# Levels 8, 16 and 32 of a block inverse: full 128x128 products against two alternating products on the diagonal 64x64 blocks

## Chip, cores and metric

One core of one Trainium2 chip. The metric is device time in microseconds of one execution, the median over the runs. The kernel computes one block of a hybrid model (a gated delta rule mixer and a convolution mixer, an output projection, a hierarchical mixture of experts, a gated embedding) over 1024 tokens of 1024 channels, all in f32 outside of a few f32r and f16 products.

## The reference, cut to what matters

The part that the change touches is the gated delta rule. For each chunk of tokens and each of 4 heads (key and value width 128) it needs the inverse of a unit lower triangular matrix:

```python
L = jnp.where(strict, jnp.einsum('bhncd,bhnsd->bhncs', k_beta, k) * decay, 0.0)
Tm = lax.linalg.triangular_solve(L + eye, eye, left_side=True, lower=True, unit_diagonal=True)
u = jnp.einsum('bhncs,bhnse->bhnce', Tm, v_beta)
w = jnp.einsum('bhncs,bhnsd->bhncd', Tm, k_beta * jnp.exp(gc)[..., None])
...
def step(S, xs_n):
    u_n, w_n, qk_n, qd_n, kd_n, gt_n = xs_n
    v_new = u_n - jnp.einsum('bhcd,bhde->bhce', w_n, S)
    o_n = jnp.einsum('bhcd,bhde->bhce', qd_n, S) + jnp.einsum('bhcs,bhse->bhce', qk_n, v_new)
    S = S * gt_n[..., None, None] + jnp.einsum('bhcd,bhce->bhde', kd_n, v_new)
    return S, o_n
```

## The kernel before

The kernel is a row of blocks that follow each other: the norm and the input projection with the two convolutions (to about 350 us), preparations of the decays, the delta rule (the block of lines 712 to 1311), the output projection with the routers (from line 1357), the routing, the experts (line 1560 on), and the last gate and norm. All engines of a block have ended before the next block begins. Within a block each engine has its own list of instructions, written out in order by hand, and they wait for each other through semaphores whose steps have names (`Steps`, line 22).

The delta rule works on tiles of 128 tokens, in 4 pairs of two tiles (g = 0, 1); every step is done for g = 0 and then for g = 1, on 4 heads at a time: an operand is `[128, 4, 128]`, and a result fills one bank of PSUM, `A[g][0]` or `A[g][1]` for the inverse, `Bk[0]` to `Bk[3]` for the rest. The inverse X of (1 + L) and its transpose Y are built up. Blocks of 8x8 are inverted column by column on VectorE (`eliminate`, line 1021), then the size of the inverted diagonal blocks is doubled level by level. Level l (3, 4, 5 for blocks of 8, 16, 32) takes ml, the part of L under the diagonal blocks that the level joins (masked by GpSimd, line 878), and does:

- U: `A[g][1] = ml^T X` on TensorE (`level_u`, line 1165), copied to `U[g]` by ScalarE (`kept`, line 786);
- X: `A[g][0] = Y^T U` (`level_x`, line 1180), and on VectorE X = X - A (`level`, line 1030);
- Y: `A[g][1] = U^T Y` (`level_y`, line 1187), and Y = Y - A on VectorE (the same function).

All matrices of these three levels have nothing outside of the two diagonal 64x64 blocks. At level 5 X is already computed for the first 64x64 block alone, since only that block of X is read afterwards. Level 6 joins the two 64x64 blocks with products of one 64x64 corner (U6, Y6), which lie partly in rows or columns 64 to 127 of the array.

PE's order for a pair is in `levels` (line 1245): U3, the turn (transpose) of the next pair's keys for g = 0, X3, Y3, the turn of the keys for g = 1, U4, X4, Y4, the turns of the queries, U5, the turns of the values, X5, Y5, KK (keys by keys of the next pair), U6, QK, Y6. Then come the solve and the state: read_state (kS), solve (of R), change (of ve), read_out, for g = 0 and 1. Line 1131 is the helper in which all these matmuls are recorded, so in the trace they are told apart by their tiles (`ps_ga<-X,ml` is U, `ps_ga<-U,Y` is X, `ps_ga<-Y,U` is Y of a level). The last pair has no next one, and so neither turns nor KK nor QK.

ScalarE's order for a pair (`levels`, line 825): U3 copies, the next keys' copies and squares (16 instructions of squares and sums), U4 copies, SiLU of the next queries and values, U5 copies, squares of the queries, U6, Y6. VectorE's order (line 1080): the subtractions of level 3, small norms, level 4, the scaled values, level 5, then on the next pair corners (d from KK, reduce, E), products (QKT, LT), the start of X8, and norm_columns; then R of the solve (line 1044).

Of the kernel before, what the change touches and what calls it, by code (L numbers as in the profile page):

```python
# [5 lines left out]
P = 128  # L6
# [5 lines left out]
ALU = mybir.AluOpType  # L12
ACT = mybir.ActivationFunctionType
# [32 lines left out]
def hybrid_block_kernel(nc, x, p, g_mix, w_in, w_conv_qkv, a_log, dt_bias, g_gdn_out, b_glu,  # L46
# [4 lines left out]
    H, DK = a_log.shape[1], g_gdn_out.shape[1]  # L51
# [24 lines left out]
    def psum(name, shape, dt=F32, ctx=None):  # L76
        return (ctx or top).enter_context(nc.psum_tensor(name, shape, dt))

    def sem(name):
        return top.enter_context(nc.semaphore(name))  # L80
# [14 lines left out]
    with top:  # L95
# [597 lines left out]
        CK = [slice(0, P // 2), slice(P // 2, P)]  # L693
        LV = (3, 4, 5)

        def both(*names):
            return [f"{n}{g}" for n in names for g in G2]

        p_one = Steps(sem("pe_one"), both("tk", "tq", "tv", "KK", "QK") + ["LR"] + both("Y8"))
        p_two = Steps(sem("pe_two"), both("U3", "X3", "Y3", "U4", "X4", "Y4", "U5", "X5", "Y5", "U6", "Y6")  # L700
                      + [f"{n}{g}" for g in G2 for n in ("kS", "AR", "dS", "o")] + both("ty"))
        a_one = Steps(sem("act_one"), both("silk", "kt", "sqk", "silq", "silv", "sqq", "y8"))
        a_two = Steps(sem("act_two"), both("U3", "U4", "U5", "U6", "Y6") + ["zs0", "zs1", "ln"]
                      + [f"va{g}" for g in G2] + both("sqo"))
        elim = [f"{n}{m}" for m in range(BS - 1, 0, -1) for n in ("et", "ex")]
        v_one = Steps(sem("dve_one"), ["ms", "rc", "bk"] + both("vb") + ["eq"] + both("c8", "cr") + ["ee"] + both("qk", "lt") + ["ec"] + elim)
        v_two = Steps(sem("dve_two"), both("X3", "Y3", "X4", "Y4", "X5", "Y5") + ["nrm"]
                      + [f"{n}{g}" for g in G2 for n in ("R", "ve", "S")] + both("on", "y"))
# [3 lines left out]
        with ExitStack() as c4:  # L712
            def two(name, shape=F4):
                return [sb(f"{name}_{g}", shape, ctx=c4) for g in G2]
# [5 lines left out]
            LT, d8, kg, X, Y, U = (two(n) for n in ("LT", "d8", "kg", "X", "Y", "U"))  # L720
            on = d8
            ml = [two(f"ml{s}") for s in G2]
# [6 lines left out]
            A = [[psum(f"ps_ga{g}{n}", F4, ctx=c4) for n in G2] for g in G2]  # L729
# [20 lines left out]
            def _(act):  # L750
# [35 lines left out]
                def kept(i, l):  # L786
                    for g in G2:
                        act.wait_ge(*p_two.sem_at(f"U{l}{g}", i))
                        if l == 3 and i:
                            act.wait_ge(*a_two.sem_at(f"sqo{g}", i - 1))  # L790
                        if l < 6:
                            nc.scalar.activation(U[g][:], A[g][1][:], ACT.Copy).then_inc(*a_two(f"U{l}{g}"))
                        else:
                            nc.scalar.activation(U[g][CK[1], :, CK[0]], A[g][0][CK[1], :, CK[1]], ACT.Copy).then_inc(*a_two(f"U{l}{g}"))

# [29 lines left out]
                def levels(i, ahead):  # L825
                    kept(i, 3)
                    if ahead:
                        keys(i + 1)
                        squares(i + 1, "k")
                    kept(i, 4)  # L830
                    if ahead:
                        turned(i + 1, "q")
                        turned(i + 1, "v")
                    kept(i, 5)
                    if ahead:
                        squares(i + 1, "q")
                    kept(i, 6)
                    corner(i)
                    gates_and_norm(i)
# [121 lines left out]
            def _(dve):  # L961
# [68 lines left out]
                def level(i, l):  # L1030
                    for g in G2:
                        dve.wait_ge(*p_two.sem_at(f"X{l}{g}", i))
                        r = (slice(0, P), slice(0, P)) if l < 5 else (CK[0], CK[0])
                        nc.vector.tensor_tensor(X[g][r[0], :, r[1]], X[g][r[0], :, r[1]], A[g][0][r[0], :, r[1]], ALU.subtract).then_inc(*v_two(f"X{l}{g}"))
                    for g in G2:
                        dve.wait_ge(*p_two.sem_at(f"Y{l}{g}", i))
                        nc.vector.tensor_tensor(Y[g][:], Y[g][:], A[g][1][:], ALU.subtract).then_inc(*v_two(f"Y{l}{g}"))

                def norm_columns(i):
                    cols = slice(2 * P * i, 2 * P * (i + 1))  # L1040
# [39 lines left out]
                def levels(i, ahead):  # L1080
                    level(i, 3)
                    if ahead:
                        norms(i + 1)
                    level(i, 4)
                    if ahead:
                        values(i + 1)
                    level(i, 5)
                    if ahead:
                        query_norms(i + 1)
                        corners(i + 1)  # L1090
                        products(i + 1)
                        start_blocks(i + 1)
                    norm_columns(i)
# [30 lines left out]
            def _(pe):  # L1124
                def heads(f):
                    for h in range(H):
                        last = f(h)
                    return last

                def mm(out, a, b, start=True, stop=True):  # L1130
                    return nc.tensor.matmul(out, a, b, start=start, stop=stop)

                def turn(i, c, g):
                    n = "qkv".index(c)
                    pe.wait_ge(*a_one.sem_at(f"sil{c}{g}", i))
                    if c == "v":
                        pe.wait_ge(*a_one.sem_at(f"kt{g}", i))
                        pe.wait_ge(*a_one.sem_at(f"sqk{g}", i))
                    elif i == 1:
                        pe.wait_ge(*v_one.sem_at(f"{'qk' if c == 'k' else 'lt'}{g}", 0))  # L1140
                    elif i:
                        pe.wait_ge(*v_two.sem_at(f"{'y' if c == 'k' else 'on'}{g}", i - 2))
                    bank = Bk[2 + g] if c == "q" else Bk[g]
                    heads(lambda h: nc.tensor.transpose(bank[:, h], qkvs[g][:, H * n + h], ident[:])).then_inc(*p_one(f"t{c}{g}"))
# [20 lines left out]
                def level_u(i, l, g):  # L1165
                    if l == 6:
                        pe.wait_ge(*v_two.sem_at(f"X5{g}", i))
                        heads(lambda h: mm(A[g][0][CK[1], h, CK[1]], LT[g][CK[0], h, CK[1]], X[g][CK[0], h, CK[0]])).then_inc(*p_two(f"U6{g}"))
                        return
                    if l == 3:  # L1170
                        pe.wait_ge(*g_one.sem_at(f"m3{g}", i))
                        if i:
                            pe.wait_ge(*a_two.sem_at(f"Y6{g}", i - 1))
                    else:
                        pe.wait_ge(*(g_one.sem_at(f"m4{g}", i) if l == 4 else g_two.sem_at(f"m5{g}", i)))
                        pe.wait_ge(*v_two.sem_at(f"X{l - 1}{g}", i))
                        pe.wait_ge(*v_two.sem_at(f"Y{l - 1}{g}", i))
                    heads(lambda h: mm(A[g][1][:, h], ml[1 if l == 4 else 0][g][:, h], X[g][:, h])).then_inc(*p_two(f"U{l}{g}"))

                def level_x(i, l, g):  # L1180
                    pe.wait_ge(*a_two.sem_at(f"U{l}{g}", i))
                    if l == 3:
                        pe.wait_ge(*a_one.sem_at(f"y8{g}", i))
                    r = (slice(0, P), slice(0, P)) if l < 5 else (CK[0], CK[0])
                    heads(lambda h: mm(A[g][0][r[0], h, r[1]], Y[g][r[0], h, r[1]], U[g][r[0], h, r[1]])).then_inc(*p_two(f"X{l}{g}"))

                def level_y(i, l, g):
                    if l == 6:
                        pe.wait_ge(*a_two.sem_at(f"U6{g}", i))
                        pe.wait_ge(*v_two.sem_at(f"Y5{g}", i))  # L1190
                        heads(lambda h: mm(A[g][1][CK[0], h, CK[0]], U[g][CK[1], h, CK[0]], Y[g][CK[1], h, CK[1]])).then_inc(*p_two(f"Y6{g}"))
                        return
                    heads(lambda h: mm(A[g][1][:, h], U[g][:, h], Y[g][:, h])).then_inc(*p_two(f"Y{l}{g}"))

                def read_state(i, g):
                    pe.wait_ge(*g_one.sem_at(f"kg{g}", i))
# [48 lines left out]
                def levels(i, ahead):  # L1245
                    n = i + 1
                    level_u(i, 3, 0)
                    level_u(i, 3, 1)
                    if ahead:
                        turn(n, "k", 0)  # L1250
                    level_x(i, 3, 0)
                    level_x(i, 3, 1)
                    level_y(i, 3, 0)
                    level_y(i, 3, 1)
                    if ahead:
                        turn(n, "k", 1)
                    level_u(i, 4, 0)
                    level_u(i, 4, 1)
                    level_x(i, 4, 0)
                    level_x(i, 4, 1)  # L1260
                    level_y(i, 4, 0)
                    level_y(i, 4, 1)
                    if ahead:
                        turn(n, "q", 0)
                        turn(n, "q", 1)
# [1114 lines left out]
```

## Time and profile before

| what | us |
|---|---|
| median of 3 runs | 1468.87 |
| runs | 1466.95 to 1472.25 |
| the profiled execution, its own time | 1466.72 |
| its span | 1465.0 |
| PE busy | 1191.1 |
| VectorE busy | 630.3 |
| ScalarE busy | 320.4 |
| GpSimd busy | 243.2 |

Times in the rows are us from the start of the span, durations of one instruction ns. PE is TensorE's matmul, PEld its weight load, which overlaps matmuls; DVE is VectorE, ACT ScalarE, POOL GpSimd. `out<-in` names the tiles, the shape behind it is rows*columns of the array in use and the size of the moving operand, xN the number of instructions. The busy time of a merged row reaches from the first start to the last end. PEclk is the granted share of the 2.4 GHz clock. A bracket at the end says how long the engine was idle before, and whom it waited for.

### The profile page before, as it was taken

What the parts mean: (1) busy time and instruction counts of PE and PEld (TensorE: products, weight loads), DVE (VectorE), ACT (ScalarE), POOL (GpSimd) and SP (SyncE); (2) the same over time, 40 slices, a digit from 0 to 9 for tenths busy, and PEclk for the clock granted to TensorE, in tenths of its full rate; (3) what the DMA queues carried; (4) which work ended last, traced back from release to release, by engine and by line L of the source; (5) the groups of instructions that cost most, each with busy time, mean ns of one, the idle gap of its engine ahead of it and who ended that gap; (6) DMA issues with size and microseconds to landing.
All of it is one profiled execution on the core that took longest, in us unless ns stands there. A gap on an engine that the chain in (4) does not pass through costs nothing. (4 is left out here: it accounts for less than half of the span.)

```text
span 1465.0 us, 16352 instructions
## 1 busy us (share of the span) xinstructions
PE 1191.1 (81%) x5812; PEld 796.7 (54%) x5812; DVE 630.3 (43%) x859; ACT 320.4 (22%) x667; POOL 243.2 (17%) x340
## 2 busy tenths in 40 slices
PE   4999999997688877799409987888788887748997
PEld 3888888885577776688303332233333232216775
DVE  7399989873466453432461111111111111135553
ACT  5221221214344423322101110000101010032222
POOL 2100000003545651000011211111112111011111
PEclk9999999967699998799659998899999999978999
DMA  4212121100000000521567799999999999952321
GB/s 146 59 43 57 43 57 43 29 1 0 1 1 1 1 1 14 182 86 72 208 253 312 317 425 426 428 422 409 413 402 417 421 410 401 397 205 82 120 94 43
DMA packets 68052, 272.57 MB, mean 186 GB/s; under 512 B 11625, under 2 KB 38442, under 8 KB 51370
## 3 DMA queue, kind: packets, MB, share of 16 engines
q1 hardware_dynamic: 56096, 254.30, 43.8%
q0 software_dynamic: 9456, 16.80, 3.0%
q10 hardware_dynamic: 2458, 0.92, 0.3%
q8 instruction: 25, 0.41, 0.1%
q14 instruction: 17, 0.14, 0.0%
HBM read 264.12 MB, written 25.43 MB: 198 GB/s over the span
## 5 line engine op out<-in xcount | busy, mean ns | idle before, releaser
L2080 PE MATMUL ps_u<-wup,xgT 128*64 128x512 f32 x1024 | 263.8, 674 | 67.5 <-DMA wup<-in_w_up_dram 65.1
L2080 PEld LDWEIGHTS ps_u<-wup,xgT 128*64 128x64 f32 x1024 | 85.9, 155 | 244.1 <-issue 242.9
L92 PE MATMUL ps_b<-n_hi,wh 128*128 128x512 f32 x384 | 150.5, 392 | 6.1 <-DVEq L405 6.1
L92 PE MATMUL ps_b<-n_lo,wh 128*128 128x512 f32 x384 | 150.3, 391 | 0.0
L92 PE MATMUL ps_b<-n_hi,wl 128*128 128x512 f32 x384 | 150.2, 391 | 0.0
L2003 DVE TENSOR_TENSOR hb<-sil,ps_u 128x256 f32<-128x256 f32 x32 | 13.5, 421 | 308.5 <-ACT sil L1943 308.5
L92 PEld LDWEIGHTS ps_b<-n_hi,wh 128*128 128x128 f32 x384 | 72.7, 189 | 21.5 <-ACTq L40 6.5
L92 PEld LDWEIGHTS ps_b<-n_hi,wl 128*128 128x128 f32 x384 | 72.6, 189 | 15.3
L92 PEld LDWEIGHTS ps_b<-n_lo,wh 128*128 128x128 f32 x384 | 72.6, 189 | 15.2
L1943 ACT ACTIVATE sil<-ps_u 128x256 f32<-128x256 f32 x32 | 12.3, 384 | 296.2 <-PE ps_u L2080 296.2
L423 DVE SCALAR_TENSOR_TENSOR convT<-upad,vecT,convT 128x1024 f32 (+1 forms) x60 | 76.8, 1281 | 0.0
L2015 DVE COPY qkvT<-ps_y 128x512 f32<-128x512 f32 x32 | 22.1, 692 | 119.7 <-PE ps_y L2101 119.7
L423 DVE SCALAR_TENSOR_TENSOR odd<-upad,vecT,odd 128x1024 f32<-128x1024 f32 x56 | 71.7, 1281 | 0.0
L1889 POOL COPY si<-sidx 128x1 int32 (+1 forms) x32 | 6.7, 209 | 389.6 <-DVE qkvT L2015 389.6
L2101 PE MATMUL ps_y<-convT,hT 128*64 128x512 f32 x256 | 60.4, 615 | 12.0 <-DVE hT L2009 12.0
L2101 PE MATMUL ps_y<-zT,hT 128*64 128x512 f32 x256 | 58.5, 598 | 11.0 <-DVE hT L2009 11.0
L357 ACT ACTIVATE wh<-wraw 128x1024 fp32r<-128x1024 f32 x24 | 25.5, 1063 | 172.6 <-PE ps_b L92 172.5
L92 PE MATMUL ps_o<-wo_hi,mix_hi 128*128 128x512 f32 x128 | 52.4, 410 | 12.6 <-DMA wr<-in_w_expert_router_dram 12.6
L601 POOL TENSOR_TENSOR GT<-sm_g,tri 128x512 f32<-128x512 f32 x8 | 8.0, 1042 | 287.2 <-DVE sm_g L657 287.2
L2069 PEld LDWEIGHTS ps_xg<-ident,xg 128*128 128x128 f32 x256 | 31.6, 195 | 44.1 <-issue 25.2
L92 PE MATMUL ps_gate<-wg_hi,hx_hi 128*128 128x512 f32 x128 | 51.7, 404 | 2.4 <-DVE hx_lo L2275 2.4
L2069 PE MATMUL ps_xg<-ident,xg 128*128 128x128 f32 x256 | 37.9, 292 | 18.8 <-DMA xg<-xn_rows,gi 18.8
(369 smaller groups left out, 2069.7 us busy)
## 6 DMA issues: line engine op xcount, KB each, us to landing
wup<-in_w_up_dram SPq DMA_DIRECT2D x64, 2048.0 KB, 16.9
zT<-in_w_down_dram SPq DMA_DIRECT2D x32, 1024.0 KB, 17.0
convT<-in_w_down_dram SPq DMA_DIRECT2D x32, 1024.0 KB, 19.0
wraw<-in_w_in_dram SPq DMA_DIRECT2D x25, 512.0 KB, 4.0
convT<-y_rows SPq DMA_DIRECT2D x16, 512.0 KB, 5.3
qkvT<-in_x_dram SPq DMA_DIRECT2D x8, 512.0 KB, 7.6
qkvT<-in_w_out_dram SPq DMA_DIRECT2D x8, 512.0 KB, 5.2
xr<-in_x_dram SPq DMA_DIRECT2D x8, 512.0 KB, 3.3
```

Of the source, the lines that this page charges most:

```text
L92: ins = nc.tensor.matmul(ps, lhs[a], rhs[b], start=first and k == 0, stop=last and k == 2)
L357: nc.scalar.activation(wh[n % 2][:], wraw[n % 2][:], ACT.Copy).then_inc(*a_proj(f"hi{n}"))
L423: ins = nc.vector.scalar_tensor_tensor(dst, src, DW(k, i), dst, ALU.mult, ALU.add)
L601: nc.gpsimd.tensor_tensor(GT[:, of_tile(t), :], sm["g"][:, t, :].unsqueeze(2).to_broadcast(F4), tri[:].unsqueeze(1).to_broadcast(F4), ALU. ...
L1889: nc.gpsimd.tensor_copy(si[k][:], sidx[:, p]).then_inc(s_idx, 1)
L1943: nc.scalar.activation(sil[k][rows], ps_u[k][rows, 0:FE], ACT.Silu).then_inc(s_sil, 1)
L2003: nc.vector.tensor_tensor(hb[k][rows], sil[k][rows], ps_u[k][rows, FE:2 * FE], ALU.mult).then_inc(s_h, 1)
L2015: nc.vector.tensor_copy(ye[k][rows, HF[1]], ps_y[rows, 1, :]).then_inc(s_y1, 1)
L2069: last = nc.tensor.transpose(ps_x[j // HJ][:, j % HJ, :], xg[k][:, j:D:NJ], ident[:])
L2080: last = nc.tensor.matmul(ps_u[k][HC[c], :], xgT[k][:, j, HC[c]], wup[k][c][:, j, :], start=j == 0, stop=j == NJ - 1)
L2101: last = nc.tensor.matmul(ps_y[HC[c], h, :], hT[k][:, f, HC[c]], wdn[k][c][:, f, HF[h]], start=f == 0, stop=f == NJF - 1)
```

## The change

The two 64x64 diagonal blocks are computed by a product each, in place of one 128x128 product. `CK` are the slices 0 to 63 and 64 to 127. In `blocks_of` the block alternates innermost: head 0 block 0, head 0 block 1, head 1 block 0 and so on. Both blocks of a result go to the same bank as before, to partitions 0 to 63 and 64 to 127. The copies and subtractions behind them become two instructions, one for each block. It applies to U3, X3, Y3, U4, X4, Y4, U5, Y5; X5 keeps its one block, level 6 is as before. No instruction changes its place in any engine's order, and no wait is added or removed.

```diff
                         if l < 6:
-                            nc.scalar.activation(U[g][:], A[g][1][:], ACT.Copy).then_inc(*a_two(f"U{l}{g}"))
+                            for c in CK:
+                                last = nc.scalar.activation(U[g][c, :, c], A[g][1][c, :, c], ACT.Copy)
+                            last.then_inc(*a_two(f"U{l}{g}"))
...
-                        r = (slice(0, P), slice(0, P)) if l < 5 else (CK[0], CK[0])
-                        nc.vector.tensor_tensor(X[g][r[0], :, r[1]], X[g][r[0], :, r[1]], A[g][0][r[0], :, r[1]], ALU.subtract).then_inc(*v_two(f"X{l}{g}"))
+                        for c in CK if l < 5 else CK[0:1]:
+                            last = nc.vector.tensor_tensor(X[g][c, :, c], X[g][c, :, c], A[g][0][c, :, c], ALU.subtract)
+                        last.then_inc(*v_two(f"X{l}{g}"))
                     for g in G2:
                         dve.wait_ge(*p_two.sem_at(f"Y{l}{g}", i))
-                        nc.vector.tensor_tensor(Y[g][:], Y[g][:], A[g][1][:], ALU.subtract).then_inc(*v_two(f"Y{l}{g}"))
+                        for c in CK:
+                            last = nc.vector.tensor_tensor(Y[g][c, :, c], Y[g][c, :, c], A[g][1][c, :, c], ALU.subtract)
+                        last.then_inc(*v_two(f"Y{l}{g}"))
...
+                def blocks_of(chunks, f):
+                    for h in range(H):
+                        for c in chunks:
+                            last = f(h, c)
+                    return last
...
-                    heads(lambda h: mm(A[g][1][:, h], ml[1 if l == 4 else 0][g][:, h], X[g][:, h])).then_inc(*p_two(f"U{l}{g}"))
+                    m = ml[1 if l == 4 else 0][g]
+                    blocks_of(CK, lambda h, c: mm(A[g][1][c, h, c], m[c, h, c], X[g][c, h, c])).then_inc(*p_two(f"U{l}{g}"))
...
-                    r = (slice(0, P), slice(0, P)) if l < 5 else (CK[0], CK[0])
-                    heads(lambda h: mm(A[g][0][r[0], h, r[1]], Y[g][r[0], h, r[1]], U[g][r[0], h, r[1]])).then_inc(*p_two(f"X{l}{g}"))
+                    blocks_of(CK if l < 5 else CK[0:1], lambda h, c: mm(A[g][0][c, h, c], Y[g][c, h, c], U[g][c, h, c])).then_inc(*p_two(f"X{l}{g}"))
...
-                    heads(lambda h: mm(A[g][1][:, h], U[g][:, h], Y[g][:, h])).then_inc(*p_two(f"Y{l}{g}"))
+                    blocks_of(CK, lambda h, c: mm(A[g][1][c, h, c], U[g][c, h, c], Y[g][c, h, c])).then_inc(*p_two(f"Y{l}{g}"))
```

## Rows read from the trace of the kernel before

**Rows 1.** The page, busy us of each engine, share of the span, instructions.

```profile
PE 1191.1 (81%) x5812; PEld 796.7 (54%) x5812; DVE 630.3 (43%) x859; ACT 320.4 (22%) x667; POOL 243.2 (17%) x340
```

**Rows 2.** Windows, the second pair and the last pair's levels: stretch, length, each engine's busy.

```profile
core 0: us, PE busy (x) PEld busy (x) DVE busy (x) ACT busy (x) POOL busy (x), PEclk, DMA share, GB/s
...
442.80:494.00 51.20, 40.60 (x333) 37.64 (x331) 28.89 (x54) 21.14 (x76) 25.37 (x25) 0.93 0.00 1
...
542.60:562.90 20.30, 20.22 (x179) 19.29 (x177) 9.72 (x15) 4.72 (x9) 7.12 (x6) 0.92 0.00 1
```

**Rows 3.** Timeline of PE, the second pair's levels: start, length, what.

```profile
442.86 1.95 PE L1131 MATMUL ps_ga<-X,ml 128*128 128x128 f32 x16
...
445.08 1.95 PE L1131 MATMUL ps_ga<-U,Y 128*128 128x128 f32 x16
...
448.66 0.60 PE L1144 MATMUL ps_gb<-ident,qkvs 128*128 128x128 f32 x4
...
452.69 2.05 PE L1131 MATMUL ps_ga<-U,Y 128*128 128x128 f32 x16 [1.64 <-ACT U L792]
...
459.99 1.14 PE L1131 MATMUL ps_ga<-U,Y 64*64 64x64 f32 x16
461.06 2.05 PE L1131 MATMUL ps_ga<-Y,U 128*128 128x128 f32 x16
462.95 1.95 PE L1131 MATMUL ps_gb<-qkvs 128*128 128x128 f32 x16
464.83 1.14 PE L1131 MATMUL ps_ga<-X,LT 64*64 64x64 f32 x16
```

**Rows 4.** Timeline of PE's weight loads, last pair, X5 and Y5.

```profile
557.33 0.54 PEld L1131 LDWEIGHTS ps_ga<-U,Y 64*64 64x64 f32 x8
...
558.69 1.86 PEld L1131 LDWEIGHTS ps_ga<-Y,U 128*128 128x128 f32 x16
```

**Rows 5.** The experts: loads and matmuls that alternate column halves (L2080), and one half (L2124).

```profile
825.07 0.14 PEld L2080 LDWEIGHTS ps_u<-wup,xgT 128*64 128x64 f32 x2 [0.28 <-issue]
825.50 0.14 PEld L2080 LDWEIGHTS ps_u<-wup,xgT 128*64 128x64 f32 x2 [0.29 <-issue]
...
824.64 6.61 PE L2080 MATMUL ps_u<-wup,xgT 128*64 128x512 f32 x30
...
L2124 PEld LDWEIGHTS ps_u<-wup_x,xgT_x x16: 132/137/137, 797.7 to 803.8; 128*64 128x64 f32 x16
L2124 PE MATMUL ps_u<-wup_x,xgT_x x16: 592/593/614, 797.8 to 804.2; 128*64 128x512 f32 x16
```

**Rows 6.** ACT in the second pair: timeline, then one group by form (busy, mean ns).

```profile
449.29 0.60 ACT L766 ACTIVATE kt<-ps_gb 128x512 f32<-128x512 f32 x1 [3.36 <-PE ps_gb L1144]
...
452.06 1.06 ACT L792 ACTIVATE U<-ps_ga 128x512 f32<-128x512 f32 x2
...
L794 ACT ACTIVATE U<-ps_ga 64x256 f32<-64x256 f32 x2 | 0.8, 380 | 3.5 <-PE ps_ga L1131 3.5
```

**Rows 7.** VectorE and GpSimd in the second pair: timeline, and one group by form.

```profile
456.11 2.50 POOL L876 TENSOR_TENSOR d<-dti,blk 128x512 f32<-128x512 f32 x2
...
460.94 0.73 DVE L1034 TENSOR_TENSOR X<-X,ps_ga 64x256 f32<-64x256 f32 x2
...
464.04 0.69 DVE L991 TENSOR_TENSOR d<-ps_gb,d 128x512 f32<-128x512 f32 x1
...
473.74 0.68 DVE L1050 TENSOR_TENSOR R<-vb,ps_gb 128x512 f32<-128x512 f32 x1
...
L1034 DVE TENSOR_TENSOR X<-X,ps_ga 64x256 f32<-64x256 f32 x2 | 0.7, 404 | 0.0
```

**Rows 8.** Timeline of PE, the last pair: U3, U5, the first read of the state.

```profile
542.61 3.29 PE L1131 MATMUL ps_ga<-X,ml 128*128 128x128 f32 x16
...
555.37 2.02 PE L1131 MATMUL ps_ga<-X,ml 128*128 128x128 f32 x16
...
562.89 1.16 PE L1131 MATMUL ps_gb<-S,kg 128*128 128x128 f32 x8
```

**Rows 9.** Windows of PE around the second pair's solve: stretch, length, busy, PEclk.

```profile
470.50:474.50 4.00, 0.64 (x3) 1.00 0.01 4
474.80:481.40 6.60, 5.82 (x28) 0.50 0.00 1
```

## The prediction

> **What bounds the kernel now.** The page first: TensorE is the busiest engine, 81% of the span [rows 1]. The chain of waits on the page reaches back only to 1318 us and never comes to the stage of the change, so the bound there has to be read from the stage itself. I cut it into windows by pairs of token tiles: the second pair takes 51.2 us with PE busy for 40.6, and the levels of the last pair, up to the first read of the state, take 20.3 us with PE busy for 20.2 [rows 2]. Then the timeline of PE in the second pair [rows 3]: read the start of each product and the gap to the next. Eight of its products in levels 3 to 5 are 128x128 ones of 16 instructions (two groups of four heads, two instructions for each f32 product): X3 and Y3 together take the 3.58 us from 445.08 to the turn at 448.66, so 1.79 each. The only wait is 1.64 us before X4, for ACT. So the levels are bound by PE's issue, but for that wait. ACT's timeline says what it is: the keys of the next pair, turned by PE after Y3, are copied and squared from 449.29 on, and the copies of U4 come behind that at 452.06 [rows 6]. X4 follows the turn of the keys by 4.03 us (448.66 to 452.69 [rows 3]), whatever PE does in between.
>
> Behind the levels VectorE takes over. From its first product with KK (464.04) to R (473.74) it is busy nearly without a gap, and R frees the solve [rows 7]. What comes before 464.04 is what the change can shorten; what comes after moves with it. The DMA share in the stage is 0.00 [rows 2] and the next stage starts when this one is over, so I carry a gain into the total one for one.
>
> **PE, instruction by instruction.** Eight products for each of four pairs go from 16 instructions of 128x128 to 32 of 64x64: 512 more matmuls and as many weight loads. X5, U6 and Y6 are such already. Sixty-four-column loads in one corner of the array start 0.058 us apart (8 in 0.54 us with a last one of 0.135), those of 128 columns 0.111 [rows 4]. If the corners took turns, a product would be 32 x 0.058 = 1.87 us against 1.79: 0.08 worse. But the change alternates the corner (rows and columns 0 to 63, then 64 to 127). No row shows that for this shape. The nearest is the expert stage, whose products alternate the column half: their loads come in twos that together last 0.14 us, one pair every 0.43 us, and 30 matmuls take 6.61 us, 0.22 each; where the same shape stays in one half, 16 start over 6.4 us, 0.43 each [rows 5]. So the second instruction of one product and the first of the next run side by side, and two corners should as well: they share neither rows nor columns. That gives 16 pairs x 0.058 = 0.93 us a product. The bounds are 0.93 and 1.87, and I take 0.93, the nearest row. The issue is no limit as far as the rows go: two loads of 137 ns each that fill 0.14 us together start within 3 ns of each other.
>
> A rule speaks against it. The Trainium skill, page "PSUM — Partial Sum Buffer", section "PSUM bank collisions raise a hardware error", says that column tiles may write one bank at once but row tiles may not, and that software has to see to it; here both corners write one bank, though in different partitions. By that rule, if the hardware held the second corner back, a product would be the 1.87 us above; no row of this case shows two row tiles.
>
> **Stops between shapes.** PE empties when the shape changes: X5 takes 1.07 us where 16 x 0.058 is 0.93, KK behind Y5 and U6 behind KK come 1.89 and 1.88 after, where 1.79 is due [rows 3]; so a stay in the small shape costs 0.14 + 0.10 + 0.09 = 0.33 us. A pair had three stays (X5, U6, Y6) and has seven with the turns and KK, QK between them; the last pair, without turns, has one in place of two.
>
> **ACT and DVE.** A copy or subtraction of 128x512 becomes two of 64x256. VectorE's two halves take 0.73 us, 404 ns each, so they start 0.32 apart, against 0.69 for a whole one, as at 464.04 [rows 7]; ACT's half is 380 ns against about 600 [rows 6], two behind each other about 0.63. I book +0.04 on each. Of 16 more instructions a pair most lie under PE, but with PE at twice the pace they no longer do, and the sum is made of the chain, not of PE's time.
>
> **The sum, pair 2.** Latencies from the rows: a consumer starts 0.2 us behind its product (VectorE at 464.04 is 1.09 after KK, whose first group takes 0.89 [rows 3, 7]), PE follows ACT in 0.03 (452.06 + 0.60, X4 at 452.69 [rows 3, 6]). From U3 = 0: the first group is issued by 0.47, the second by 0.94; ACT copies 0.70 to 1.32 and to 1.85. Turn of keys at 1.13 to 1.57, X3 1.71 to 2.65, Y3 to 3.59, second turn at 3.78. Before it was 5.80 (448.66 less 442.86). Saved: 2.0. U4 now waits for VectorE (four subtractions of 0.64 each from 2.4 on, the third done by 4.5), but lies in front of the 4.03 us of ACT's chain, so X4 comes at 7.8 in place of 9.83. From X4 = 0: Y4 done 1.9, turn of queries 2.1 to 3.0, U5 3.1 to 4.05, turn of values 4.25 to 5.1, X5 (unchanged) 5.25 to 6.2, Y5 to 7.1, KK at 7.3. Before 10.26 (462.95 less 452.69). Saved: 2.9. GpSimd's masked table, which VectorE's first product with KK reads, was done 5.9 us after X4 (456.11 + 2.50 [rows 7]); it is wanted at 8.4 now, 11.35 before, so it doesn't decide. So 4.9 us a pair, 14.7 for three. From KK on nothing changes in the order or the work.
>
> **Last pair.** From U3 to the first read of the state it takes 20.28 us (542.61 to 562.89 [rows 8]), U3 to U5 12.76 of it with the first product at half clock. New: a level lasts 4.2 us (0.94 for U, ACT to 1.3, X from 1.35, VectorE's X0, X1, Y0 from 2.05 to 4.1), with about 5.1 for level 3 at half clock, 3.3 for level 5, and 2.4 for level 6 and the way out: 15.0. Saved: 5.3.
>
> Together 14.7 + 5.3 = 20.0 us. Against the profiled execution (1466.72) that is 1446.7; it lies 2.15 below the median, so **1449** on the median's scale.
>
> **Rivals.**
> (a) The pairs overlap in part: something common to both corners (weight reads, the bank) spaces the instructions at about 0.045 us. A product is 1.44, seven on the path save 2.4 a pair, the new stops take 1.2 back: about 5 us in all, **1463**, from 1456 to 1468. For it: no row has two f32 loads of 64 every 58 ns. Against: loads in the expert rows lie side by side at 137 ns each, as long as alone.
> (b) The other side: the corners take turns. Seven products on the path lose 0.08 each (U4 hides in ACT's chain), and 1.2 us of stops a pair come on top: 1.75 a pair, 0.3 in the last, +5.6: **1474.5**. The point from which it decides is a pace of 50 ns an instruction: there (1.79 - 1.60) x 7 = 1.3 just pays for 1.2 us of stops. For it: the bank is shared by two row tiles. Against: the partitions are not, and the expert rows.
> (c) Changing the corner empties PE as changing the shape does: 16 changes of 0.1 to 0.2 us a product, about 2.4 us x 29 products: some 70 us, **1539**. Nothing shows it; the expert rows show the contrary for columns.
> (d) The clock. It falls to 0.50 behind 4 us in which PE was busy for 0.64 [rows 9]. PE now pauses more: 2.3 us before X4, about 1 in a level. If the grant stayed at 1.2 GHz through the levels, each product cost 0.93 more and the turns and KK 4.4 a pair, some 34 us with what the chain still hides, less the 20: **1483**. Against: 1.64 us of pause with few products around it did not drop it. One more or one less half-clock stretch in the solves, 1 to 3 us, is in the forecast's own range.
>
> **Chances.** Forecast 0.66 (1444 to 1456: 3 us either way for a stretch of half clock in the solves that comes or goes, 2 us for the latencies of the chain, which I rounded, and 2 more on the slow side, where each of 64 more ACT and VectorE instructions adds to it), (a) 0.14, (b) 0.10, (c) 0.05, (d) 0.05. The range 1444 to 1468 holds the first two, 0.80. A measurement of this kernel can tell about 0.3%, 4.4 us, from no change. Faster: the forecast and most of (a), 0.78; the same: the rest of (a) and the milder half of (b), 0.07; slower: 0.15.
>
> **What would show it.** In the timeline of PE each changed product as 32 instructions of 64*64 in about 1.1 us; loads in twos; turn of keys 3.8 us after U3, X4 4.0 after that with a longer wait for ACT, KK 7.3 after X4; new waits of U4 for VectorE's Y; VectorE unchanged from its first product with KK to R; stops of 0.33. The stage shorter by about 20 us, every later stage as long as before. Wrong: 32 instructions in 1.87 us or more, or PEclk under 0.9 within the levels.

## The result, and the profile after

| kernel | median us | runs | stage of the delta rule, profiled execution |
|---|---|---|---|
| before | 1468.87 | 5 | 203.0 |
| changed | 1459.60 | 5 | 199.4 |

The ratio is 0.9939 with a 95% interval of 0.9918 to 0.9959: faster by 9.3 us, where 20 were forecast. The profiled execution of the changed kernel took 1463.44 us (span 1461.6), the slowest of its five, so it shows more of the loss than the median does. "The stage" is measured here, for every kernel, from the first U3 of the first pair to the first matmul of the output projection. What follows the stage took 869 to 874 us in the profiles of this study, though no edit touches it, so the stage leaves out a spread that the medians carry. But a stage is one execution, and repeats of it differ too (199.4, 195.8 and 195.8 for the changed kernel).

The page of the changed kernel, busy us of each engine: PE lost 12.2 us, VectorE and ScalarE gained 7.4 and 4.8 [rows 1].

```profile
PE 1178.9 (81%) x6324; PEld 779.2 (53%) x6324; DVE 637.7 (44%) x899; ACT 325.2 (22%) x691; POOL 240.2 (16%) x340
```

The windows of the changed kernel for the second pair and the last pair's levels, as in [rows 2]:

```profile
442.50:493.50 51.00, 39.58 (x459) 34.93 (x458) 30.30 (x63) 22.58 (x82) 25.32 (x24) 0.83 0.00 1
542.50:559.40 16.90, 14.08 (x307) 12.58 (x305) 10.74 (x25) 5.66 (x15) 7.06 (x6) 0.90 0.01 2
```

The second pair is 51.0 us, where it was 51.2: nothing of the 4.9 us forecast for it arrived. From U3 to KK (the part that the forecast shortened) it took 19.00 in place of 20.09; from KK to the next U3, where the forecast had nothing change, 31.97 in place of 31.07. In the first and third pair that second part is longer too, by 3.1 and 1.4 us. The last pair's levels fell from 20.3 to 16.9, where 15.0 was forecast. And PEclk of the second pair went from 0.93 to 0.83. The timeline of PE says where (start, length, what, and in brackets the idle time before with its releaser); changed kernel, second pair:

```profile
441.50 1.12 PE L1254 MATMUL ps_gb<-ident,d 128*128 128x128 f32 x4 [1.84 <-DVE d L1079]
442.54 1.98 PE L1136 MATMUL ps_ga<-X,ml 64*64 64x64 f32 x32
444.45 1.11 PE L1155 MATMUL ps_gb<-ident,qkvs 128*128 128x128 f32 x4
445.49 1.94 PE L1136 MATMUL ps_ga<-U,Y 64*64 64x64 f32 x32
447.25 1.11 PE L1136 MATMUL ps_ga<-Y,U 64*64 64x64 f32 x32
448.29 0.66 PE L1155 MATMUL ps_gb<-ident,qkvs 128*128 128x128 f32 x4
449.42 0.68 PE L1136 MATMUL ps_ga<-X,ml 64*64 64x64 f32 x16 [0.47 <-DVE Y L1041]
...
452.55 1.47 PE L1136 MATMUL ps_ga<-U,Y 64*64 64x64 f32 x32 [1.57 <-ACT U L793]
453.86 1.72 PE L1136 MATMUL ps_ga<-Y,U 64*64 64x64 f32 x32
455.50 1.97 PE L1155 MATMUL ps_gb<-ident,qkvs 128*128 128x128 f32 x8
457.40 1.18 PE L1136 MATMUL ps_ga<-X,ml 64*64 64x64 f32 x32
...
461.55 2.05 PE L1136 MATMUL ps_gb<-qkvs 128*128 128x128 f32 x16
```

And its windows of PE in the same stretches (length, busy, PEclk):

```profile
440.50:447.20 6.70, 5.70 (x72) 0.50 0.00 1
447.40:454.00 6.60, 4.26 (x108) 1.00 0.01 2
454.20:457.40 3.20, 3.20 (x35) 0.50 0.00 0
```

Read them together. A product at 2.4 GHz (Y3 at 447.25, U5 at 457.40) is what the forecast said, 32 instructions in about 1.1 us. The second turn of the keys comes 5.75 us after U3 (3.8 forecast), because U3, the turn and X3 ran at 1.2 GHz. X4 follows it by 4.26 (4.0 forecast), its wait for ACT's U is there, and U4 waits for VectorE's Y, also as forecast. KK follows X4 by 9.00 (7.3 forecast), because most of Y4 and the turn of the queries ran at 1.2 GHz again. X4 itself ran at full clock; its 1.47 us hold a wait of its second tile for ACT, whose four half copies take 1.54 us. The kernel before has PEclk 1.00 in all of 442.8 to 463.0. In the changed one two such half-clock stretches are there in every pair with turns (the first one of the first pair, up to 396, is in the kernel before as well): from 396 to 560 its clock is halved for 44.4 us, that of the kernel before for 17.3 (in the solves and the last U3), summed over the stretches of the granted clock.

One more row was not as forecast. Changed kernel, last pair, timeline of VectorE at level 4, where nothing else runs on it:

```profile
550.54 1.73 DVE L1036 TENSOR_TENSOR X<-X,ps_ga 64x256 f32<-64x256 f32 x4 [1.53 <-PE ps_ga L1136]
552.30 1.73 DVE L1041 TENSOR_TENSOR Y<-Y,ps_ga 64x256 f32<-64x256 f32 x4
```

Four halves start 0.44 us apart, not 0.32 as the two X5 passes do in [rows 7], and PE waits behind them for as long:

```profile
553.30 0.68 PE L1136 MATMUL ps_ga<-X,ml 64*64 64x64 f32 x16 [0.99 <-DVE Y L1041]
```

So a level of the last pair takes 5.03 us (548.27 to 553.30), 4.2 forecast.

Two theories for the missing 10 us came out of this. **P (passes)**: a half pass on the other partitions doesn't overlap the one before it, so that split passes on ACT and VectorE cost time on the chain of waits. **C (clock)**: the faster products leave PE idle for longer beside VectorE and ACT, it has less to do between, and the clock falls in two more places of a pair. The rival of both was that the products only look fast, and that something about changing the corner (rivals a to c of the prediction) costs the time.

### The profile page after: what moved, and what is told of

Read it like the earlier page. It is cut to its first block and busy times, and to the rows that moved or that the text cites. A ratio compares the mean times of both kernels' runs of the same rounds, so it can differ in the third digit from the quotient of the medians.

```text
span 1461.6 us, 17440 instructions
## 1 busy us (share of the span) xinstructions
PE 1178.9 (81%) x6324; PEld 779.2 (53%) x6324; DVE 637.7 (44%) x899; ACT 325.2 (22%) x691; POOL 240.2 (16%) x340
## 5 line engine op out<-in xcount | busy, mean ns | idle before, releaser
L92 PEld LDWEIGHTS ps_b<-n_lo,wh 128*128 128x128 f32 x384 | 72.7, 189 | 15.1
L92 PEld LDWEIGHTS ps_b<-n_hi,wl 128*128 128x128 f32 x384 | 72.7, 189 | 15.1
L1954 ACT ACTIVATE sil<-ps_u 128x256 f32<-128x256 f32 x32 | 12.2, 383 | 296.6 <-PE ps_u L2091 296.6
L2080 PEld LDWEIGHTS ps_xg<-ident,xg 128*128 128x128 f32 x256 | 31.6, 195 | 43.9 <-issue 25.2
L2080 PE MATMUL ps_xg<-ident,xg 128*128 128x128 f32 x256 | 37.9, 292 | 18.6 <-DMA xg<-xn_rows,gi 18.6
## 6 DMA issues: line engine op xcount, KB each, us to landing
convT<-in_w_down_dram SPq DMA_DIRECT2D x32, 1024.0 KB, 19.1
```

The source lines that it names most:

```text
L92: ins = nc.tensor.matmul(ps, lhs[a], rhs[b], start=first and k == 0, stop=last and k == 2)
L1954: nc.scalar.activation(sil[k][rows], ps_u[k][rows, 0:FE], ACT.Silu).then_inc(s_sil, 1)
L2080: last = nc.tensor.transpose(ps_x[j // HJ][:, j % HJ, :], xg[k][:, j:D:NJ], ident[:])
```

## The experiments

Behind each median stands the ratio to runs of the kernel before on the same chip, with its 95% interval; those runs had a median of 1469.44, 1466.58 and 1468.79 us in the three batches.

**The changed kernel again**, as a base for the first batch.

> The changed kernel once more, for a second profile. Clock theory: the corners run side by side (0.93 us a product at full clock), and most of the missing gain lies in stretches of half clock inside the levels, where TensorE now pauses or works with a quarter of its rows and columns. Then the span moves with the time spent at half clock: 1456 to 1464, with the first U product or X4 and Y4 of most pairs at 1.47 to 1.98 us in place of 1.10. Rival (the passes of ScalarE and VectorE): the levels are as long whatever the clock does, and the spread between executions is small.

1460.44 us, 0.9922 (0.9895 to 0.9950); stage 195.8. The gain stands. Runs in the last batch gave 1459.98, 0.9934 (0.9914 to 0.9953), stage 195.8.

> The changed kernel, beside the two with fillers on one chip, so that what the clock costs it and the kernel before can be set against each other. Clock theory (the change itself brings half clock into the levels): changed less changed with fillers exceeds before less before with fillers by 4 to 8 us. Rival (the half clock was there before, in the solves, and the fillers take it away from both alike): the two differences agree within 2 us.

The three pairs with turns took 18.4 to 19.1 us from U3 to KK in all three profiles. What the second expectation asked is answered with the fillers below.

**Block by block in place of alternating.**

```diff
-                    for h in range(H):
-                        for c in chunks:
+                    for c in chunks:
+                        for h in range(H):
```

> The changed kernel with the loops of blocks_of swapped: the four heads of block 0, then those of block 1. If the alternation is what makes two matmuls run side by side: 32 instructions a product at 0.058 us each, 1.87 us, TensorE without pauses and so at full clock, 1473 to 1480. If the 64x64 shape alone made the products fast: the time of the changed kernel, 1457 to 1463.

1481.21 us, 1.0077 (1.0048 to 1.0107), 21 us slower than with alternation; stage 215.3. Its timeline of PE, second pair:

```profile
448.49 0.36 PE L1136 MATMUL ps_ga<-Y,U 64*64 64x64 f32 x1
448.59 0.31 PE L1136 MATMUL ps_ga<-U,Y 64*64 64x64 f32 x1
448.65 0.31 PE L1136 MATMUL ps_ga<-Y,U 64*64 64x64 f32 x1
...
461.89 1.54 PE L1136 MATMUL ps_ga<-X,ml 64*64 64x64 f32 x32
...
465.37 1.49 PE L1136 MATMUL ps_ga<-Y,U 64*64 64x64 f32 x32
```

A product took 1.5 us at full clock, more than 1.1 and less than the 1.87 of corners in turn. At 448.49 to 448.65 the records of Y3, which begins in the other corner, stand between those of X3, which comes first in the program: where the corner changes, the next one's instructions start early. The expectation of full clock failed: part of this kernel's loss is the clock (half for 13.7 of the 23.0 us from U3 to KK in the second pair, and for all but a little of the last pair's levels). What it settles: the alternation is what makes a product 1.1 us, and the two corners do run side by side. The rival falls.

**Half passes alone**, in the kernel before: VectorE's subtractions in two halves, ACT's copies whole, the products full 128x128.

```diff
...
-                        nc.vector.tensor_tensor(Y[g][:], Y[g][:], A[g][1][:], ALU.subtract).then_inc(*v_two(f"Y{l}{g}"))
+                        for c in CK:
+                            last = nc.vector.tensor_tensor(Y[g][c, :, c], Y[g][c, :, c], A[g][1][c, :, c], ALU.subtract)
+                        last.then_inc(*v_two(f"Y{l}{g}"))
```

> The kernel before, with only VectorE's subtractions of X and Y split in two 64x256 passes (128x128 products, ScalarE's copies whole). Pass theory: the second half, on other partitions, starts only when the first has ended (0.425 us apart, not the 0.32 that I took), and costs little here, since TensorE is the bound: +0.5 to +3 us. Rival (the split itself eats the gain): +6 us or more.

1471.15 us, 1.0004 (0.9987 to 1.0021): no difference; stage 206.1, with half clock for 6.4 us more of it than in the kernel before (203.0). The passes got longer all the same, to 1.74 us for four, while PE's next product follows without a wait:

```profile
448.06 1.74 DVE L1034 TENSOR_TENSOR X<-X,ps_ga 64x256 f32<-64x256 f32 x4 [2.37 <-PE ps_ga L1134]
```

So the halves cost what they cost with any product, and PE at its old pace hides most of it (a level of the last pair took 5.80 us, 5.63 before).

**Whole passes in the changed kernel.** Products as in the change, but ACT and VectorE copy and subtract 128x512 at once. For that the bank must hold zeros outside of the blocks, so U3 of the first tile, and in the first pair of both, stays a 128x128 product.

```diff
-                            for c in CK:
-                                last = nc.scalar.activation(U[g][c, :, c], A[g][1][c, :, c], ACT.Copy)
-                            last.then_inc(*a_two(f"U{l}{g}"))
+                            nc.scalar.activation(U[g][:], A[g][1][:], ACT.Copy).then_inc(*a_two(f"U{l}{g}"))
...
+                    if l == 3 and (g == 0 or i == 0):
+                        heads(lambda h: mm(A[g][1][:, h], m[:, h], X[g][:, h])).then_inc(*p_two(f"U3{g}"))
+                        return
```

> The changed kernel with whole 128x512 passes on ScalarE and VectorE; so that the parts outside of the diagonal blocks are zero, U3 of the first tile (and in the first pair of both) stays a 128x128 product. Pass theory: VectorE's four passes of a level take 2.5 us in place of 3.5; the last pair's levels gain 0.8 us each, the other pairs 0.5 at the first product with KK, less 0.4 a pair for U3: 1455 to 1458. Clock theory alone: no change beyond what the clock does, 1457 to 1463.

1454.56 us, 0.9875 (0.9848 to 0.9903), 5.9 under the changed kernel of the same batch; stage 191.6, where the three profiles of the changed kernel gave 195.8 to 199.4. A level of the last pair takes 4.13 us in place of 5.03, at full clock in both, so theory P stands. The 5.9 us are not its price, for the intervals of the two ratios overlap, and in this profile the clock was halved for less of the levels too (3.4 us from U3 to KK in the second and third pair, 8 in the changed kernel).

**Keeping PE busy.** Products of the identity with itself, of no use to the result, are put where PE waits in the first three pairs: 11 ahead of the solve's R, 5 and 7 ahead of the two turns of the output (their tile is d in the trace) that stand in front of U3, and 5 ahead of X4. They go to banks that are free there; the wait for R now stands behind its 11 fillers.

```diff
+                def fill(bank, k):
+                    for _ in range(k):
+                        mm(bank[:, 0], ident[:], ident[:])
...
+                            fill(Bk[1], 11)
...
+                    if ahead:
+                        fill(A[0][0], 5)
...
+                        fill(A[1][1], 5)
...
+                    if ahead:
+                        fill(A[1][1], 7)
```

In the changed kernel:

> The changed kernel with products of the identity with itself (128x128, 0.22 us each at full clock, results overwritten unread) put into TensorE's waits of the first three pairs: 5 before X4, 11 before the solve's R, 5 and 7 before the two turns of the output. They do no useful work and are sized to end before the wait does. Clock theory: the half clock between the first U3 and the last pair falls from about 45 us to under 15, U3, X4 and Y4 take 1.10 us in every pair, each pair's levels 15.5 to 16.5 us in place of 19.0 and the way from R to the next U3 18.1 in place of 20.2: 1446 to 1451. Rival (the waits, not the clock, set the time): 1458 to 1464, as without them.

and in the kernel before, since that has half-clock stretches too:

> The same fillers in the kernel before, as a control. Clock theory: it had 17 us of half clock there, most of them hidden or in the solves, so the fillers give 1 to 4 us: 1465 to 1468. If fillers gained as much here as in the changed kernel, the clock would not be what the change has cost.

1451.06 us, 0.9902 (0.9886 to 0.9918) for the changed kernel, 1460.11, 0.9958 (0.9943 to 0.9973), for the one before. The second expectation failed: 1 to 4 us were forecast for the kernel before, and it gained 6.5. The clock stays up in both. Windows from about X3 of the first pair to the first read of the state in the last; changed kernel, changed with fillers, before, and before with fillers:

```profile
396.00:558.00 162.00, 124.91 (x1610) 110.56 (x1606) 99.49 (x210) 69.46 (x252) 80.24 (x73) 0.86 0.01 2
```

```profile
396.00:540.90 144.90, 127.41 (x1787) 114.33 (x1784) 98.24 (x211) 70.24 (x253) 82.59 (x73) 1.00 0.01 2
```

```profile
396.20:562.80 166.60, 136.94 (x1148) 127.41 (x1146) 93.63 (x172) 65.95 (x234) 82.59 (x73) 0.95 0.00 1
```

```profile
396.20:556.00 159.80, 147.51 (x1308) 139.07 (x1307) 94.24 (x172) 65.78 (x232) 81.34 (x73) 1.00 0.01 1
```

The changed kernel wins 17 us of this stretch by more PE work, the one before 7. Both were measured once more, beside the changed kernel in one batch, so that the medians can be subtracted:

> e5 once more, beside the changed kernel: 1449 to 1453. The levels of pairs 1 and 2 at 16.2 us and of the last pair at 16.1.

> e6 once more, beside the kernel before: 1459 to 1462. The levels of pairs 1 and 2 at 20.1 us, those of the last pair at 18.7.

1450.24 (0.9879, 0.9853 to 0.9906) and 1462.85 (0.9959, 0.9944 to 0.9975), with 1459.98 for the changed kernel and 1468.79 for the one before. So the fillers gain 9.7 us in the changed kernel and 5.9 in the one before. The difference, 3.8 us, would be what the change itself loses by the clock, but the medians do not settle it: it lies between the two answers that were expected (4 to 8, or within 2), and it is a difference of four medians whose ratios have intervals of 2 to 4 us either way. The stages put it higher: 14.0 us (195.8 to 181.8) against 6.5 to 8.1 (203.0 to 194.9 and 196.5). Much of the gap between 14.0 and 9.7 lies behind the stage, where both profiles of the changed kernel with fillers took 874.2 us and the three without 870.3 to 870.7; why was not tried. With fillers in both kernels the change gains 12.6 us in this batch, 9.1 in the one before it, and 13.1 and 14.7 by the stage.

What settles it is the same stretch in every profile. "Levels" is U3 to KK in the three pairs with turns plus U3 to the first read of the state in the last pair; beside it stands the rest of the three pairs. All in us, read from the timelines of PE:

| kernel | levels | KK to the next U3, three pairs |
|---|---|---|
| before | 82.6 | 88.3 |
| before with fillers (two profiles) | 81.0, 81.1 | 83.7, 84.9 |
| changed (three profiles) | 73.7, 72.9, 72.9 | 93.8, 92.9, 91.0 |
| changed with fillers (two profiles) | 66.2, 66.0 | 83.6, 85.8 |
| changed, whole passes and fillers (below) | 61.0 | 84.0 |

In the levels the fillers give the changed kernel 6.7 to 7.7 us and the one before 1.5 to 1.6. So theory C stands: the half clock inside the levels came with the change, and costs 5 to 6 us there.

**Both repairs**, whole passes and fillers:

> The changed kernel with whole passes (e4) and the fillers. If the two losses, clock and split passes, are separate, they add: the levels of a pair 14.5 to 15.5 us, 1442 to 1448. If they are one and the same, no faster than the better of the two alone.

1442.74 us, 0.9838 (0.9824 to 0.9852): 24 us faster than the kernel before (0.0162 x 1467), the fastest of the study; stage 175.5. Of these 24 us the change has 17.4, since the kernel before with the same fillers took 1460.11 in this batch. Its timeline of PE, second pair, to be laid beside [rows 3]:

```profile
438.46 1.67 PE L1131 MATMUL ps_ga<-X,ml 128*128 128x128 f32 x24
...
442.65 0.66 PE L1154 MATMUL ps_gb<-ident,qkvs 128*128 128x128 f32 x4
...
446.75 1.16 PE L1131 MATMUL ps_ga<-U,Y 64*64 64x64 f32 x32 [0.76 <-ACT U L792]
```

and of VectorE, level 4 of the last pair:

```profile
531.60 1.28 DVE L1034 TENSOR_TENSOR X<-X,ps_ga 128x512 f32<-128x512 f32 x2 [1.65 <-PE ps_ga L1131]
532.80 1.28 DVE L1037 TENSOR_TENSOR Y<-Y,ps_ga 128x512 f32<-128x512 f32 x2
```

The same elements in 1.28 us that took 1.73 in four passes. From U3 to KK the three pairs take 16.06, 15.45 and 15.46 us (15.1 forecast), and a level of the last pair 4.13 (4.2 forecast). With the passes by blocks and fillers it was 17.69, 16.18 and 16.18, and 5.03. The passes are thus worth 0.7 us a pair and 2.1 in the last pair (16.14 to 14.06 from U3 to the read of the state), some 4.3 us in all; the rest of the first pair's difference is clock.

**The same without the filler ahead of X4:**

```diff
-                        fill(A[0][0], 5)
+                        fill(A[0][0], 0)
```

> e7 without the 5 fillers before X4. If the wait of TensorE before X4 is what drops the clock for X4 and Y4, those two take 1.7 to 1.97 us in most pairs and the time is 2 to 4 us above e7; if the pauses of the solve before the levels drop it, X4 and Y4 stay at 1.10 and the time is that of e7 within 1 us.

1444.83 us, 0.985 (0.9833 to 0.9867); stage 182.5, which is 7.0 more, while the medians differ by only 2.1 with intervals that overlap. U3 to KK took 19.11, 16.78 and 15.44 us: in this execution most of X4 and Y4 ran at half clock in the first two pairs and not in the third. So without a filler ahead of X4 the clock can fall there although the other fillers keep it up before, but it does not always: the wait was 2.06, 2.05 and 2.06 us. In the kernel before, a wait of 1.64 us at the same place, between products of nearly twice the length, did not drop it in any pair of its profile [rows 3], where 1.31 us in the first pair of the changed kernel were followed by a half-clock stretch. The length of the wait alone does not decide.

**Is it two instructions, or other partitions?** The passes of the kernel with both repairs are split again, on ACT and VectorE, now by heads: 128x256 twice, on the same partitions.

```diff
-                            nc.scalar.activation(U[g][:], A[g][1][:], ACT.Copy).then_inc(*a_two(f"U{l}{g}"))
+                            for hh in (slice(0, H // 2), slice(H // 2, H)):
+                                last = nc.scalar.activation(U[g][:, hh], A[g][1][:, hh], ACT.Copy)
+                            last.then_inc(*a_two(f"U{l}{g}"))
```

> e7 with each whole pass split again in two, but by heads (128x256, all partitions) in place of by blocks (64x256). As many instructions as in the changed kernel. If the change of partitions is what keeps the second half from starting early: halves 0.33 us apart, a level of the last pair 4.3 us, levels of a pair 15.7, 1443 to 1445. If two instructions without a semaphore between them are the cause: 0.42 us apart, a level of 5.0, 1449 to 1452.

1445.73 us, 0.9845 (0.9821 to 0.9870), where passes by blocks took 1450.24 in the same batch; stage 179.9. VectorE, level 4 of the last pair:

```profile
534.01 1.42 DVE L1037 TENSOR_TENSOR X<-X,ps_ga 128x256 f32<-128x256 f32 x4 [1.64 <-PE ps_ga L1137]
535.34 1.41 DVE L1042 TENSOR_TENSOR Y<-Y,ps_ga 128x256 f32<-128x256 f32 x4
```

Eight passes in 2.74 us, so one starts every 0.33 or so, as in the forecast's row; by partitions it was every 0.44. A level of the last pair takes 4.38 us, against 4.13 with whole passes and 5.03 with passes by blocks. Most of the cost is the change of partitions, a quarter or so ((4.38 - 4.13) / (5.03 - 4.13) = 0.28) the number of instructions.

## Why the prediction was right and wrong

**PE, instruction by instruction: right.** 0.93 us a product was taken, and 32 instructions in 1.10 to 1.15 with the last one's length is what stands in the products at full clock that have no wait inside. The kernel with blocks apart shows that it comes from the alternation. The rule of the Trainium skill that spoke against it (page "PSUM — Partial Sum Buffer", section "PSUM bank collisions raise a hardware error") did not bite: two row tiles wrote one bank in different partitions, and neither held the other back (1.10 us for 32 instructions). Rivals (a), (b) and (c) fall with it.

**Stops between shapes: about right.** KK, in between two stays, comes 1.98 us before U6 (461.55 to 463.53), 1.79 being due, which is the 0.19 that the step had. X5 and Y5 now share a shape and overlap.

**ACT and DVE: wrong, the first failing step.** "I book +0.04 on each" took the pace of two halves from [rows 7]. Those are the two X5 passes, of tile 0 and tile 1, both on partitions 0 to 63. The new second half lies on partitions 64 to 127, and starts only about when the first ends: 0.44 us apart. A level's X takes VectorE 1.73 us in four halves in place of 1.28 in two whole passes, so a split pass costs (1.73 - 1.28) / 2 = 0.22 and not 0.04, and Y costs the same again; in the last pair that shows whole in the wait of the next U for Y (a level of 5.03 us against 4.13). The term is worth 4.3 us by the timelines with the clock up; the medians put 5.9 on it without fillers and 8.3 with them (1451.06 less 1442.74), which hold clock and spread besides. The step's own sentence, that PE at twice the pace hides them no more, was right, and the kernel with half passes alone shows its other side: under full products they cost no time that the medians show.

**The clock: put at nothing in the levels, the second failing step.** Rival (d) had the mechanism, with products and turns at half clock behind longer waits, but as all or nothing: 0.05 for a clock that stays down, and "one more or one less half-clock stretch in the solves, 1 to 3 us" in the forecast. What came is between: two stretches in every pair with turns, one from the turns of the output through X3 and one over Y4 and the turn of the queries, at the same places each time. The argument against it, that 1.64 us of pause with few products around it had not dropped the clock, was taken from a kernel in which those products took nearly twice as long. The change loses 5 to 6 us by it in the levels, read from the timelines, and 6 to 7.5 in the stage; the 3.8 of the medians is not clear of their noise. The sign for it was written down ("PEclk under 0.9 within the levels") and is what the profile shows.

**The sum, pair 2, and Last pair.** With both costs removed the sum's arithmetic holds: 15.45 us from U3 to KK against 15.1, 4.13 a level against 4.2, and the levels of all pairs 82.6 to 61.0, 21.6 less where 20.0 were forecast (1.6 of it is half clock that the kernel before had in its last pair, 20.28 against 18.71 us with fillers). In the changed kernel the second pair saved 1.1 us in its levels (20.09 to 19.00) in place of 4.9, and the last pair 3.5 in place of 5.3. The levels together saved 8.9 to 9.7 of the 20, and 4.3 for the passes with 5 to 6 for the clock make up nearly all that is missing there.

**"From KK on nothing changes": right for the work, wrong for the time.** From KK to the next U3 the three pairs take 91.0 to 93.8 us together, 88.3 before. In the profile of the result the way from KK to the solve is 1.36, 0.24 and 1.35 us longer, of which 1.1 each in the first and third pair is a VectorE pass that came out long (last section), and the way from there to U3 1.7, 0.7 and 0.1, with half clock for 8.9, 8.7 and 3.4 us in place of 3.4, 6.8 and 3.4. This loss changes from execution to execution. The rest of the program is as long as before, as forecast.

## What to carry to other kernels

Work taken from the bottleneck engine is not only saved there: read what the shorter work no longer hides (short passes on the other engines) and whether the granted clock holds through the waits that get relatively longer, for here the two together took about half of the gain. When a duration of a new instruction is taken from a row, take care that the row agrees in what lies between two instructions too, here the partitions and not only the shape. If PE's waits sit beside short products and PEclk falls there, a few useless products in the waits are a cheap test and may be kept; here they gained 6 us in the kernel before and 10 in the changed one, by the medians.

## What the runs showed of the hardware, unexpected

- A VectorE pass that starts on other partitions than the one before it does not overlap it (0.44 us apart at a length of 0.42), where one on the same partitions does (0.33 apart). ScalarE does the same: four copies of 64x256 take 1.54 us where they alternate blocks, (1.54 - 0.38) / 3 = 0.39 apart at a length of 0.38; those of 128x256 on the same partitions start 0.28 apart.
- Matmuls of another corner can start ahead of earlier ones in the program (in the timeline of the kernel with blocks apart the first record of Y3 stands ahead of the last three of X3), so that even corners that aren't alternated overlap a little: 1.5 us a product, not 1.87.
- One VectorE pass of 128x1024 between KK and R takes 1.21 or 2.33 us in the same kernel, from pair to pair, and what goes with it is GpSimd's mask beside it. Kernel before, first and second pair:

```profile
421.38 3.58 POOL L879 TENSOR_TENSOR ml<-LT,lev 128x512 f32<-128x512 f32 x2 [10.64 <-PE ps_gb L1131]
422.62 1.21 DVE L1041 TENSOR_TENSOR convT<-convT,vr 128x1024 f32<-128x1024 f32 x1
...
470.25 2.49 POOL L879 TENSOR_TENSOR ml<-LT,lev 128x512 f32<-128x512 f32 x2 [10.63 <-PE ps_gb L1131]
471.49 2.33 DVE L1041 TENSOR_TENSOR convT<-convT,vr 128x1024 f32<-128x1024 f32 x1
```

  GpSimd's second mask starts within 0.02 us of the pass in all 42 pairs with turns of the fourteen profiles. In 30 of them the pass is long and the mask takes 1.26 to 1.28 us; in the other 12 the pass is short and the mask takes 2.35 to 2.37. In the last pair, with no mask beside it, the pass takes 1.22 or 1.23 in all fourteen. So one of the two stands for about 1.1 us while the other works; which one it will be is not shown, and no run moved them apart. The pass stands on the path to R, so it is worth 1.1 us a pair. It was long in one pair of three before, in two or three of three in the changed kernel, and in one to three with fillers: part of the spread of the stage, and no effect of the change that these runs could show.
